# Attention probabilities turned by a product with a diagonal of inverse sums, instead of being scaled first and then turned by the identity

## What is computed

```python
# layer 0
m = max(max(scores), sink)
p = exp(scores - m)
probs = p / (sum(p) + exp(sink - m))
out = einsum('bnhgqk,bnkhd->bnqhgd', probs, vv)
# layer 1
s = where(sel_ok, q . k_sel * HEAD_DIM ** -0.5, -inf)
out = softmax(s) . v_sel
```

## Time and profile before

| | |
|---|---|
| median of 3 runs | 1124.03 us (1121.41 to 1128.97) |
| the profiled execution | 1121.3 us |
| its span, first to last instruction | 1119.5 us |
| TensorE busy | 1077.3 us, 96% of the span |
| VectorE, ScalarE, GpSimd busy | 743.7, 542.5, 192.6 us |
| mean granted TensorE clock | 0.988 |

### The profile page before, as it was taken

The page is one execution under the profiler, slowest core; times in us unless marked ns, Lnnn a source line. Parts: engine busy times, 40 slices in busy tenths (PEclk is TensorE's granted clock), DMA queues, the critical chain, the costliest instruction groups (busy, mean ns, idle before and its releaser), DMA issues. The chain is left out here.

```text
span 1119.5 us, 14906 instructions
## 1 busy us (share of the span) xinstructions
PE 1077.3 (96%) x5433; PEld 865.6 (77%) x5433; DVE 743.7 (66%) x1284; ACT 542.5 (48%) x1014; POOL 192.6 (17%) x338
## 2 busy tenths in 40 slices
PE   7999999999999999999989978999999999999996
PEld 6766678988888888888667755668988888888885
DVE  4354544577688697687478878644587698696684
ACT  6376653445435444435454466653445444444431
POOL 1344530000000000005312368440000000000004
PEclk9999999999999999999999989999999999999998
DMA  7431403824445455422433314003734455355401
GB/s 229 94 77 38 99 16 73 172 62 102 101 106 111 85 113 113 91 61 49 94 76 76 76 39 113 2 1 83 163 71 102 90 113 113 77 112 113 99 15 76
DMA packets 50793, 97.84 MB, mean 87 GB/s; under 512 B 4448, under 2 KB 4640, under 8 KB 50720
## 3 DMA queue, kind: packets, MB, share of 16 engines
q1 hardware_dynamic: 50208, 96.78, 38.7%
q10 hardware_dynamic: 512, 0.11, 0.0%
HBM read 94.78 MB, written 2.10 MB: 87 GB/s over the span
## 5 line engine op out<-in xcount | busy, mean ns | idle before, releaser
L1920 PE MATMUL bank<-r_hi,w_hi 128*128 128x512 f32 (+1 forms) x456 | 177.5, 389 | 0.0
L1921 PE MATMUL bank<-r_hi,w_lo 128*128 128x512 f32 (+1 forms) x456 | 177.4, 389 | 0.0
L1922 PE MATMUL bank<-r_lo,w_hi 128*128 128x512 f32 (+1 forms) x456 | 177.4, 389 | 0.0
L1536 DVE TENSOR_TENSOR w_lo<-w_raw,w_hi 128x1024 fp32r<-128x1024 f32 x84 | 102.1, 1223 | 70.7 <-ACT w_hi L1082 70.6
L1082 ACT ACTIVATE w_hi<-w_raw 128x1024 fp32r<-128x1024 f32 x84 | 87.7, 1055 | 118.8 <-PE bank L1922 82.9
L2261 PE MATMUL bank<-w_hi,hid_hi 128*128 128x512 f32 x336 | 130.7, 389 | 0.0
L2262 PE MATMUL bank<-w_lo,hid_hi 128*128 128x512 f32 x336 | 130.7, 389 | 0.0
L2263 PE MATMUL bank<-w_hi,hid_lo 128*128 128x512 f32 x336 | 130.7, 389 | 0.0
L1091 ACT ACTIVATE w_hi<-w_raw,gT 128x512 fp32r<-128x512 f32 x96 | 64.6, 716 | 107.6 <-DMA w_raw<-in_w_mlp_up 76.1
L776 POOL TENSOR_TENSOR acc<-acc,G 128x512 f32<-128x512 f32 x8 | 13.0, 1653 | 594.3 <-ACT waste L950 594.3
L1930 PE MATMUL bank<-w_hi,r_hi 128*128 128x512 f32 x240 | 101.4, 423 | 5.2 <-DVE w_lo L1313 3.5
(11 more groups left out here) (198 smaller groups left out, 2135.7 us busy)
## 6 DMA issues: line engine op xcount, KB each, us to landing
w_raw<-in_w_mlp_up SPq DMA_DIRECT2D x64, 512.0 KB, 6.5
w_raw<-in_w_mlp_down SPq DMA_DIRECT2D x64, 512.0 KB, 6.9
w_raw<-in_b_w_in SPq DMA_DIRECT2D x16, 512.0 KB, 6.5
w_raw<-in_a_w_in SPq DMA_DIRECT2D x8, 512.0 KB, 6.5
w_raw<-in_a_w_out SPq DMA_DIRECT2D x8, 512.0 KB, 5.9
w_raw<-in_b_w_out SPq DMA_DIRECT2D x8, 512.0 KB, 6.2
X<-in_x SPq DMA_DIRECT2D x4, 512.0 KB, 6.6
w_raw<-in_a_w_in SPq DMA_DIRECT2D x8, 256.0 KB, 7.3
```

What stands on the lines that cost most here:

```text
L1536: nc.vector.tensor_tensor(half_of(w_lo[:, u % 2, :], a), b_of(PRODUCTS[i][1], a), half_of(w_hi[:, u % 2, :], a).bitcast(f32), ALU.subtract ...
L1920: nc.tensor.matmul(bank, whi, xhi, start=start, stop=False)
L1921: nc.tensor.matmul(bank, wlo, xhi, start=False, stop=False)
L1922: return nc.tensor.matmul(bank, whi, xlo, start=False, stop=stop)
```

## The change

GpSimd no longer touches the probabilities. For each turn it makes four 128x128 diagonal matrices, the identity times the inverse sums of a head (`inverses`, in the place of `normed`), into a new tile `diag` with two places. `diag` lies on bytes that `yg` and a raw weight buffer of the MLP use at other times. A place of `diag` is written once the blocks of the turn before the last are turned, which is a new wait of GpSimd on `pt_ready`. TensorE turns and normalises at once: the instruction of `transposes` is an ordinary fp32 product of the block of `probs` with `diag`, where it was a transposition by the identity. The operand that is loaded as weights (the block of `probs`) is the same, and so are the bank, the waits and the counts of semaphores.

```diff
+        diag = at("diag", [2, 4, P], f32, offset[0])
...
-            def normed(layer, n):
+            def inverses(layer, n):
+
                 N = 16 * layer + n
-                W = width(layer, turn(layer, n)[1])
                 pool.wait_ge(inv_done, N + 1)
+                if N >= 2:
+                    pool.wait_ge(pt_ready, PT_AT[N - 1])
                 for c in range(4):
-                    v = probs[:, N % 3, c, 0:W]
-                    nc.gpsimd.tensor_tensor(v, v, inv_sum[:, N % 3, c:c + 1].to_broadcast([P, W]), ALU.mult).then_inc(p_done, 1)
+                    nc.gpsimd.tensor_tensor(diag[:, N % 2, c, :], ident[:, 0:P], inv_sum[:, N % 3, c:c + 1].to_broadcast([P, P]),
+                                            ALU.mult).then_inc(p_done, 1)
...
-                        normed(layer, n)
+                        inverses(layer, n)
...
-                    ins = nc.tensor.transpose(bank[:, blk(e)], probs[:, N % 3, e, blk(c)], ident[:, 0:P])
+                    ins = nc.tensor.matmul(bank[:, blk(e)], probs[:, N % 3, e, blk(c)], diag[:, N % 2, e, :], start=True, stop=True)
```

## The result

The changed kernel takes 1141.07 us (median of 4 runs, 1139.44 to 1148.1) beside 1122.82 for the kernel before: a ratio of 1.0176, with a 95% interval of 1.0151 to 1.0201. A second set, on one chip with 15 runs of the kernel before, gave 1143.24 (1142.61 to 1143.87) beside 1122.16: 1.0186 (1.0172 to 1.0200). The change costs 20 to 21 us.

A forecast was written before the change was run, and what follows sets the result against it. TensorE was taken to bound the kernel, with waits only around layer 1's attention and in layer 0's. Added product time 29.6 us less 7.4 taken back by waits gives 22.2 over 1121.3: 1143.5 us, range 1131 to 1157.

The forecast's parts named there:

- GpSimd's part: GpSimd's work on probabilities: some 33 us saved, off the path apart from the chain before layer 1's weight split.
- TensorE's product, 29.6 us: 272 turned blocks in both attentions: two records of 0.109 us where there was one, 29.6 us added.
- What the waits take back, 7.4 us: TensorE's waits in attention shrink as products run meanwhile: 2.2 us in layer 0, 2.6, 1.75 and 0.87 in layer 1.
- the rotary wait in layer 1: TensorE's wait for GpSimd's rotary step in layer 1: eight transpositions counted before it, about 0.9 us shorter.
- ring: Before 700.5 us in layer 1, VectorE's masks and TensorE's scores wait for each other: half of 16 counted, 0.87 us.
- The clock, taken at nothing: TensorE's clock in both attentions: no change counted, though at most 10.4 us of work is lost there at half rate.
- The stretch between the attentions, taken as unchanged: From layer 0's attention to layer 1's, first MLP included: no term in the sum; MLPs to last as before.
- The new wait, costed at nothing: GpSimd's wait on `pt_ready` before writing diagonals: asks for blocks turned an iteration earlier, so costed at nothing.
- Rival 1 (the clock): More records keep TensorE's clock up in attention: up to 8.5 us return, 1135 us; chance 0.12.
- Rival 2 (loads show): Products' weight loads aren't hidden: 0.280 us a block, +46.5, waits take about 9, 1159 us; chance 0.11.
- Rival 3 (a record doesn't shrink with its columns): Product's two records cost 0.215 us each, 0.43 a block: +87, less 9, 1199 us; chance 0.03.
- Rival 4 (not slower): Product's second record costs under 0.027 us, waits cover it, GpSimd's chain gains: 1119 to 1120 us; chance 0.06.

The follow-up runs named there:

- Experiment 4: Kernel before with each transposition issued twice into the same place, as many records as the product has: 1140.84 us, 1.0165.
- experiment 6: Kernel before with the change in layer 0 alone: 1130.96 us, 1.0069; with it in layer 1 alone: 1133.35 us, 1.0104.
- the second kernel of experiment 8: Kernel before with four more VectorE instructions of the mask's kind put inside GpSimd's weight split: 1130.46 us, 1.0083.
- experiment 8: VectorE's mask beside GpSimd's weight split: kernel before, mask delayed 1128.76 us, four instructions added 1130.46; changed kernel, split waiting for the mask 1143.21.
- experiments 2 and 3: Kernel before with only TensorE's fp32 product by the identity: 1143.36 us, 1.0183; with only GpSimd's diagonals, blocks still transposed: 1123.04 us, 1.0006.
- experiment 3: Kernel before with GpSimd's part alone: diagonals made, blocks still transposed by the identity, normalisation left out: 1123.04 us, 1.0006.
- experiment 5: Changed kernel with exponentials and diagonal written as fp32r, so each product is one single-pass record: 1127.92 us, 1.0048.

## Why the prediction was right

It gave 1143.5 us, made up as 29.6 - 7.4 = 22.2 us over 1121.3. The measured cost is 20 to 21 us. What carried it is right: the product is two records a block, each of the length that the earlier trace rows gave, GpSimd's part is off the path, and the dense stages pay. That it came within 2.5 us is in part luck: four terms were off, by 1.5 to 5.7 us, and nearly cancel. Point by point:

- *TensorE's product, 29.6 us.* Two records a product: right (544). The distance was 0.1115 us instead of 0.109, which I worked out from the starts of the instructions in the timeline. What the step missed is at the head of a group. The product's weight load lasts 192 ns (median) where the transposition's lasts 140, and the first two records of a group start 0.213 us apart where it was 0.168; that fits a first load with nothing to hide under. By groups: 24 groups of eight cost 2.05 - 1.09 = 0.96 more, 20 of four 1.16 - 0.66 = 0.50, in all 33.0 us. The term was 3.4 us too small. Experiment 4, which has the records without the longer load, came out 2.4 us below the product.
- *What the waits take back, 7.4 us.* They gave 8.9 (18.7 to 9.8). Layer 1 gave 5.2, the sum that was counted, but not by the waits that were counted: the rotary wait in layer 1, which was to shrink by 0.87, stayed at 2.1 us. Layer 0 gave 3.7 for 2.2 counted. In layer 1 the stretch with the key rounds takes up everything, ring and all, since VectorE sets its pace (experiment 6).
- *The clock, taken at nothing.* This step was wrong. By the earlier trace rows the lower clock took 0.03 x 117 + 0.10 x 69 = 10.4 us of full-rate work in the attentions before; in the same stretches after it took 0.01 x 124 + 0.05 x 69 = 4.7. So the clock gave back 5.7 us there. The stretches add up with it: 33.0 - 8.9 - 5.7 = 18.4, against 18.3 measured (layer 0's attention ends 7.0 us later, layer 1's takes 131.3 us for 120.0). Some of the 5.7 may be the execution's: the second kernel of experiment 8, unchanged there, ends layer 0's attention at 168.8 us instead of 171.5.
- *The stretch between the attentions, taken as unchanged.* It was 3.2 us longer, with a clock of 0.91 over 40 us. The lower clock there comes and goes with nothing changed ahead of it (experiment 8): the profile before caught an execution without it, both profiles after one with it. Whether the change makes it more frequent no run tells. With it 18.3 + 3.2 = 21.5, against 21.3 between the two profiled executions.
- *The clock over many executions.* Mean 0.986 to 0.990 before, 0.989 to 0.995 in the second set after. In the runs of these sets the kernel before took 1123.7 to 1124.6 us in its six executions at 0.985 or 0.986, and 1120.3 to 1122.1 in the fourteen at 0.989 or 0.990. That is some 3 us for 0.0035; by that the gain of 0.003 is about 2.5 us, an estimate, and what is left of 5.7 less 3.2 is the same.
- *GpSimd's part.* Off the path, as said: experiments 2 and 3. The 1.4 us at the weight split were real and shortened layer 1's attention by 1.4 us (experiment 3), but the stretch between the attentions took them back. The new wait, costed at nothing because it asks for old work, did hold GpSimd for 9.2 us at one place, in the dense part (until 733.4 us), which the prediction had named as a sign of being wrong. It cost nothing all the same: TensorE waited 0.3 us for a diagonal, once, as before.
- *The MLPs as they were.* 352.2 us from layer 1's attention to the end in both, and the first MLP unchanged.
- *Rival 1 (the clock).* In the attentions it came by two thirds, 5.7 of its 8.5 us; of that 3.2 went again between them. The rule of the Trainium skill behind it (TensorE: Matmul & The Clock Gate, Part 4: PE-mode transpose), that transpositions don't count as activity for the clock, isn't borne out: doubling the transpositions left the mean clock at 0.990 to 0.992, as high as the products did (experiment 4).
- *Rival 2 (loads show).* True at the head of a group only, 0.045 us at 44 places.
- *Rival 3 (a record doesn't shrink with its columns).* Wrong for fp32 from 256 to 128 columns, where the prediction's 0.109 held. But one pass instead of two made it no shorter (experiment 5).
- *Rival 4 (not slower).* Wrong; TensorE's cost per product was 0.12 us where 0.027 was the limit.

What the prediction didn't have is the collision of experiment 8. In the two profiled executions the mask starts at the same time (683.77 and 683.80 us) and the last product of L2110 5.4 us apart (784.8 and 779.4); 3.9 of these are TensorE's waits for VectorE's masks (5.9 for 2.0 us). It took one execution to 1148.1, inside the range.

## What to carry to other kernels

Count the records of an operation on the bounding engine before the work that it saves on another: a plain fp32 product by a diagonal is two records where a transposition is one, and 33 us saved on GpSimd, for which TensorE waited 1.7 us in two places (and for its rotary step, which the change leaves alone), paid nothing back that the time shows. Price added work by stages: the stage with VectorE's rounds took up all of it, the dense stages paid every record. And where a moved or shortened GpSimd instruction comes to lie beside a VectorE instruction on SBUF alone, look at that instruction's longest duration, not its mean. Lay a stretch that the change doesn't touch side by side too: here one of 466 us moved by 3 us between executions, as much as a term of the sum.

## What the runs showed of the hardware that I had not expected

- A record with a 128-column load and 128 moving columns starts 0.109 to 0.112 us after the one before it, as an fp32 transposition, as half of an fp32 product and as a single-pass fp32r product, though fp32r records of 512 columns take 0.23, which would be 0.06 for 128.
- The product's weight loads last 192 ns in the median, the transposition's 140, with the same operand; it shows only at the head of a group (0.213 instead of 0.168 us to the second record).
- A VectorE TENSOR_SCALAR on 384 columns took 0.36 us with GpSimd idle (experiment 8), 0.45 to 0.68 in three executions with GpSimd at work on shorter instructions or at the end of one, 1.30 to 1.36 beside its 1.28 us instructions, and 5.99 once.
- The mean clock was 0.981 with 272 single-pass records in attention, about 0.988 with 272 transpositions, about 0.991 with 544 records of either kind and 0.996 with 1088. More records also meant shorter waits, and no run separates the two.
- The granted clock over the same 40 us of the same work was 1.00 in one execution and 0.91 in another, and the stretch around it 3 us longer.
